# Branch A's values: both halves of V in one stationary operand, half the rows moved and added afterwards

## The reference, cut to what matters

```python
qa, ka = apply_rope(qa), apply_rope(ka)
o_a, _ = banded_attention(qa, ka, va, A_WINDOW - 1, sink=sinks)       # softmax over at most 128 keys
y_a = ((o_a * silu(gate_a)) @ w_pa)
y_b = ((o_b * silu(gate_b)) @ w_pb)                                   # branch B, dilated attention
merged = sigmoid(mg_a + b_gate[0]) * y_a + sigmoid(mg_b + b_gate[1]) * y_b
out = layer_norm(DN_ALPHA * x + merged @ w_out, ln_g, ln_b)
```

## Time and profile before

| | |
|---|---|
| time, median of 3 runs | 1389.39 us (1388.9 to 1390.16) |
| the profiled execution's own time | 1388.75 us |
| its span, from the first to the last instruction | 1387.0 us |
| mean granted TensorE clock | 0.997 |
| PE, DVE, ACT, POOL busy | 98%, 34%, 41%, 48% of the span |

### The profile page before, as it was taken

The page is one execution under the profiler, slowest core; times in us unless marked ns, Lnnn a source line. Parts: engine busy times, 40 slices in busy tenths (PEclk is TensorE's granted clock), DMA queues, the critical chain, the costliest instruction groups (busy, mean ns, idle before and its releaser), DMA issues.

```text
span 1387.0 us, 19876 instructions
## 1 busy us (share of the span) xinstructions
PE 1360.5 (98%) x6488; PEld 1154.3 (83%) x6488; DVE 477.4 (34%) x846; ACT 574.5 (41%) x971; POOL 669.8 (48%) x512
## 2 busy tenths in 40 slices
PE   9999999999999999999999999999999999999996
PEld 7888888778988988898898888888888888888884
DVE  5866565652031223203111011010101202287688
ACT  5455464543472365347237322222222222445442
POOL 4633443454555545455454465464555636422214
PEclk9999999999999999999999999999999999999998
DMA  8432241435374354337434343653536446377664
GB/s 260 131 122 76 76 136 52 130 111 119 93 168 137 87 120 135 119 92 163 147 110 137 88 149 113 151 129 102 177 91 157 122 130 147 95 248 259 208 241 152
DMA packets 204990, 190.07 MB, mean 137 GB/s; under 512 B 16528, under 2 KB 178576, under 8 KB 204944
## 3 DMA queue, kind: packets, MB, share of 16 engines
q1 hardware_dynamic: 191344, 151.74, 37.1%
q0 software_dynamic: 13600, 37.75, 11.0%
HBM read 185.23 MB, written 41.94 MB: 164 GB/s over the span
## 4 chain that ended last, share of the span: by engine, by line
PE 50%; issue 25%; POOL 20%; DVE 2%; ACT 1%; DMA 1%; POOLq 0%; SPq 0%; DVEq 0%; ACTq 0%
PE acc L1493 45%; POOL w_lo L574 11%; POOL w_lo L573 9%; PE ps_scores L1493 2%; PE ps_out L1493 1%; PE ps_turn L1493 1%; PE ps_out L1582 0%; DMA raw<-xT 0%; DMA raw<-w_in 0%; DVE w_lo L1290 0%; POOL q_left L599 0%; POOL q_left L601 0%; DVE x_lo L981 0%; DVE z L1351 0%; ACT both_stats L655 0%
## 5 line engine op out<-in xcount | busy, mean ns | idle before, releaser
L573 POOL TENSOR_TENSOR w_lo<-raw,w_hi 128x512 fp32r<-128x512 f32 x241 | 319.3, 1325 | 700.8 <-ACT w_hi L627 577.3
L1493 PE MATMUL acc<-x_hi,w_hi 128*128 128x512 f32 x1216 | 478.2, 393 | 5.8 <-POOL w_lo L574 3.2
L1493 PE MATMUL acc<-x_hi,w_lo 128*128 128x512 f32 x1216 | 474.2, 390 | 0.0
L1493 PE MATMUL acc<-x_lo,w_hi 128*128 128x512 f32 x1216 | 474.1, 390 | 0.0
L627 ACT ACTIVATE w_hi<-raw 128x1024 fp32r<-128x1024 f32 x224 | 234.5, 1056 | 337.2 <-PE acc L1493 332.5
L574 POOL TENSOR_TENSOR w_lo<-raw,w_hi 128x512 fp32r<-128x512 f32 x241 | 332.4, 1379 | 0.0
L1493 PEld LDWEIGHTS acc<-x_hi,w_hi 128*128 128x128 f32 x1216 | 228.5, 188 | 51.2 <-POOL w_lo L574 3.9
L1493 PEld LDWEIGHTS acc<-x_hi,w_lo 128*128 128x128 f32 x1216 | 228.2, 188 | 48.3
L1493 PEld LDWEIGHTS acc<-x_lo,w_hi 128*128 128x128 f32 x1216 | 228.5, 188 | 44.1
L1216 DVE TENSOR_TENSOR part_a<-acc,part_a 128x512 f32<-128x512 f32 x16 | 11.1, 691 | 321.7 <-PE acc L1493 321.7
L1493 PE MATMUL acc<-w_hi,x_lo 128*128 128x384 f32 x256 | 85.6, 334 | 0.0
(11 more groups left out here) (265 smaller groups left out, 1621.3 us busy)
## 6 DMA issues: line engine op xcount, KB each, us to landing
raw<-w_in SPq DMA_DIRECT2D x384, 128.0 KB, 2.3
q_left<-w_out POOLq DMA_DIRECT2D x12, 2048.0 KB, 13.6
raw<-w_in SPq DMA_DIRECT2D x256, 96.0 KB, 2.5
raw<-q_left SPq DMA_DIRECT2D x32, 512.0 KB, 4.8
raw<-w_in SPq DMA_DIRECT2D x64, 192.0 KB, 2.9
raw<-w_pa SPq DMA_DIRECT2D x64, 128.0 KB, 6.2
raw<-w_out SPq DMA_DIRECT2D x16, 512.0 KB, 4.2
raw<-xT SPq DMA_DIRECT2D x8, 512.0 KB, 4.7
```

The source lines that it names most:

```text
L573: nc.gpsimd.tensor_tensor(dst[:, left], raw[:, slot, left], hi[:, left].bitcast(F32), ALU.subtract)
L1493: ins = nc.tensor.matmul(into[:, 0:cols], s, m, start=start and k == 0, stop=stop and k == n - 1)
```

## The change

Branch A's values no longer sit twice in a stationary operand. `v_pair` holds, in its 128 columns, the rounded half of the 64 channels and beside it the remaining half. One matmul with a piece of the probabilities gives the rounded half's product in rows 0 to 63 and the remaining half's in rows 64 to 127. Two passes follow each other, over `probsT_hi` and over `probsT_lo`, instead of three matmuls for each block of keys; the wait for `probsT_lo` moves between the passes. The result is the sum of the upper and the lower rows. ACT copies, for each head of the pair, the 64 rows that lie on the wrong side into `across` (`move_halves`, at the plan's "values"), DVE adds the rows that lie on the right side, and then multiplies by the gate, 128 x 128 at once. The product lo x lo is now contained too.

```diff
-        v_hi_a, v_lo_a = (at(n, branch_at + where, [P, 4, A_KV, P], F32R)
-                          for n, where in (("v_hi_a", 8192), ("v_lo_a", 12288)))
+        v_pair = at("v_pair", branch_at + 8192, [P, 4, A_KV, P], F32R)
+        across = at("across", branch_at + 12288, [P, 2, P])
...
+        def v_part(c):
+
+            return v_pair.rearrange("p b v (c d) -> p (b v) c d", c=2)[:, :, c, :]
 
         def turned_v():
-
-            return ps_turn.rearrange("p (n d) -> p n d", d=A_DH).unsqueeze(2).to_broadcast([P, 8, 2, A_DH])
+            return ps_turn.rearrange("p (n d) -> p n d", d=A_DH)
...
+            def move_halves(u, a):
+
+                act.wait_ge(out_psum, a + 1)
+                if u > 1:
+                    act.wait_ge(gated_a, a - 1)
+                for hh in range(2):
+                    main, rest = (slice(A_DH * n, A_DH * n + A_DH) for n in (hh, 1 - hh))
+                    last = nc.scalar.activation(across[main, u % 2, :], ps_out[rest, hh * P:hh * P + P], ACT.Copy)
+                last.then_inc(halves_moved, 1)
...
+                    if stage == "values" and kind == "a":
+                        move_halves(u, first_unit + u)
...
-                        nc.scalar.activation(twice(v_hi_a), turned_v(), ACT.Copy).then_inc(v_hi_ready, 1)
+                        nc.scalar.activation(v_part(0), turned_v(), ACT.Copy).then_inc(v_hi_ready, 1)
...
             def gate_out(kind, u, a, i):
 
-                dve.wait_ge(out_psum, a + 1)
+                dve.wait_ge(halves_moved, a + 1)
                 j, b = divmod(u, 4)
                 for hh in range(2):
-                    g = gate_a[half[hh], j, b * P:(b + 1) * P]
-                    last = nc.vector.tensor_tensor(g, ps_out[half[hh], hh * P:hh * P + P], g, ALU.mult)
+                    whole = across[half[hh], u % 2, :]
+                    last = nc.vector.tensor_tensor(whole, ps_out[half[hh], hh * P:hh * P + P], whole, ALU.add)
                 last.then_inc(out_gated, 1)
+                dve.wait_ge(out_gated, a + 1)
+                g = gate_a[:, j, b * P:(b + 1) * P]
+                nc.vector.tensor_tensor(g, across[:, u % 2, :], g, ALU.mult).then_inc(gated_a, 1)
                 if b == 3 and j == 1:
-                    dve.wait_ge(out_gated, a + 1)
+                    dve.wait_ge(gated_a, a + 1)
                     split_gated(kind, gate_a[:, j, :], i + A_ITERS * j, i * 2 + j)
...
-            nc.vector.tensor_tensor(twice(v_lo_a), turned_v(), twice(v_hi_a).bitcast(F32), ALU.subtract).then_inc(v_a_ready, 1)
+            nc.vector.tensor_tensor(v_part(1), turned_v(), v_part(0).bitcast(F32), ALU.subtract).then_inc(v_a_ready, 1)
...
                         if kind == "a":
-                            pe.wait_ge(probsT_rest, a + 1)
                             if u:
                                 pe.wait_ge(out_gated, a)
...
-                            for kb in kbs:
-                                for n, (v, p) in enumerate(((v_hi_a, probsT_hi), (v_hi_a, probsT_lo), (v_lo_a, probsT_hi))):
-                                    last = nc.tensor.matmul(ps_out[:, 0:2 * P], v[:, b - 1 + kb, j, :],
+                            for p in (probsT_hi, probsT_lo):
+                                if p is probsT_lo:
+                                    pe.wait_ge(probsT_rest, a + 1)
+                                for kb in kbs:
+                                    last = nc.tensor.matmul(ps_out[:, 0:2 * P], v_pair[:, b - 1 + kb, j, :],
                                                             p[:, 2 * kb:2 * kb + 2, :].rearrange("p c q -> p (c q)"),
-                                                            start=kb == kbs[0] and n == 0, stop=kb == 1 and n == 2)
+                                                            start=p is probsT_hi and kb == kbs[0], stop=p is probsT_lo and kb == 1)
```

More of the change, by code:

```diff
@@ L335, in build @@
         out_psum, out_gated = sem("out_psum"), sem("out_gated")
+        halves_moved, gated_a = sem("halves_moved"), sem("gated_a")
         collected, weighed, near_spread, mixed = sem("collected"), sem("weighed"), sem("near_spread"), sem("mixed")
@@ L364, in by_residue @@
             return t.rearrange("p (r b j) -> p r b j", b=4, r=NR)
-        def twice(t):
-            return t.rearrange("p b v (c d) -> p (b v) c d", c=2)
+        def v_part(c):
+            return v_pair.rearrange("p b v (c d) -> p (b v) c d", c=2)[:, :, c, :]
         def turned_v():
-            return ps_turn.rearrange("p (n d) -> p n d", d=A_DH).unsqueeze(2).to_broadcast([P, 8, 2, A_DH])
+            return ps_turn.rearrange("p (n d) -> p n d", d=A_DH)
         def slot_o(q):
@@ L1134, in attend @@
                 if kind == "a" and g == 15:
-                    dve.wait_ge(out_gated, first_unit + A_UNITS // 2)
+                    dve.wait_ge(gated_a, first_unit + A_UNITS // 2)
                     split_gated(kind, gate_a[:, 0, :], i, i * 2)
```

## The result

The changed kernel takes 1400.51 us (median of 6 runs, 1396.54 to 1402.64), the kernel before 1389.73 us (6 runs, 1388.9 to 1390.16) beside it: ratio 1.0075, 95% interval 1.006 to 1.009, slower. The profiled execution took 1400.09 us, with a span of 1398.3 and a mean granted clock of 0.992, where it was 0.997. The forecast was 1395.4 us, slower: right in sign, inside its range, 5.1 us too low.

The account below looks back on a forecast made before the run. PE, busy 98% of 1387 us, was taken as the bound. Terms -5.9 (matmuls), +9.0 (stage ends), +2.4 (DVE stalls) and +0.5 (fourth stage's end) gave +6.0 us: 1389.39 becomes 1395.4, range 1389 to 1403.5.

Parts of the forecast that it names:

- matmuls, with unit 0's wait: Branch A's values on PE: 46 matmuls save 5.4 us, one more per stage inside unit 0's wait 0.5; together -5.9.
- units 2 and 3, hand-over: DVE late after units 0 and 1, stalling PE: +2.4 us over four stages; fourth stage's end, towards branch B: +0.5.
- three stage ends: DVE's gate waits for ACT's late copy of unit 7, scores 3.0 us later per end: +9.0 us (6.0 to 12.3).
- rival +6: Clock falls to 1.2 GHz after PE's idle time at three stage ends, 2 us each: 1401.4; chance 22%.
- What comes off PE: Branch A's values: 56 fewer matmuls at 0.117 us, ten at stage ends not counted, leaving 46, 5.4 us.
- The hand-over: Fourth stage's end, where branch B takes over: later gate and new multiplication delay the rotary work, +0.5 us (0 to 1.4).
- the last rival: Faster: ACT's late copy at stage ends is hidden and unit 7's matmuls count, -6.6 us, 1382.8; chance 9%.
- the first rival: PE idle about 3.4 us before three stages lowers the clock, 2 us lost each: 1401.4 (to 1406); chance 22%.
- The second rival: VectorE binds the units: multiplication meets POOL at most units, stalls reach 1.7 us per stage: 1399.8; chance 8%.
- No change and faster: Stage ends: chain free of POOL, 1389.9, no change, chance 11%; or ACT's copy hidden, 1382.8, faster, chance 9%.
- the late chain: DVE's delayed work at stage ends runs free of POOL: +2.0 us per end, +0.5 in all, 1389.9; chance 11%.

Follow-up runs that it names:

- e1: Changed kernel without ACT's move and DVE's addition, the halves not summed, only the 56 fewer matmuls kept: 1382.96 us, ratio 0.9953 to the kernel before.
- e6: Changed kernel with unit 7 of each stage gated as before, without move and addition, its halves not summed: 1386.71 us, ratio 0.9983 to the kernel before.
- e3: Changed kernel with 32 unused transposes of the identity on PE during the wait at each of three stage ends: 1395.66 us, ratio 1.0046 to the kernel before.
- e5: Changed kernel with unit 7's move ahead of bank 0's swap and the two q_low operations at blocks 7 and 10 instead of 5 and 8: 1386.88 us.
- e2: Changed kernel with unit 7's move put ahead of bank 0's swap in ScalarE's queue at three stage ends: 1389.08 us, ratio 0.9996 to the kernel before.
- e10: Changed kernel with unit 7's move between bank 0's swap and the next `high` in ScalarE's queue: 1396.77 us, ratio 1.0051 to the kernel before.
- e4: Changed kernel with a third value pass, the rounded probabilities again, and the wait ahead of all passes: 1402.3 us, ratio 1.0091 to the kernel before.

## Why the prediction came out as it did

| term | predicted | measured | from |
|---|---|---|---|
| matmuls, with unit 0's wait | -5.9 | -6.6 | e1 - before |
| units 2 and 3, hand-over | +2.4 + 0.5 | +3.75 | e6 - e1 |
| three stage ends | +9.0 | +8.95 | e3 - e6 |
| the clock | 0, rival +6 | +4.85 | changed - e3 |
| sum | +6.0 | +11.0 | beside its own kernel before: +10.8 |

By the starts the four terms are -7.2, +4.4, +8.8 and +4.8, together +10.8.

- **What comes off PE**: right in kind, 0.7 short. The step failed by which unit 7's six matmuls "don't count", since "what follows there is set by DVE": DVE's chain begins with the result of those matmuls. In e1 the stages that end this way shrink by 1.9, and its -6.6 us is what the last rival gives if unit 7's matmuls count.
- **Units 2 and 3**: DVE's lateness came where it was placed, but once in a stage: at unit 2 in three of them, at unit 3 in the fourth. By starts the recorded 2.2 us are 0.6 in each of the three and 1.2 in the fourth, 3.0 in all; of the 0.8 by which e6's three stages are longer than e1's, 0.2 remain unplaced.
- **The hand-over**: mis-sized by little. Stage 4 is 0.5 longer in e3 than before, with 14 fewer matmuls, of which the prediction lets 10 count; it holds the fourth `probs_a` wait of 0.9 and a new one of 1.2 for `shifted`, against 0.4 less for `q_a`. The table parts them: e5, without the `probs_a` wait, is still 0.9 longer in stage 4 than e1 (52.9 and 52.0). That is the hand-over, with what little the other units lose there; 0.5 was predicted.
- **The stage ends**: the step that decided, right in place and in size: PE waits 3.28 us, 3 to 3.6 were predicted. By starts 58.7 - 55.8 = 2.9 per end, 3.0 predicted; ACT's two copies 0.54, the 0.55 predicted; the multiplication 0.41 and the cast 1.27 beside POOL, as the chain had it. e2 and e10 show that it was the place in ScalarE's queue.
- **The clock**: the step that failed. "The mechanism at a stage's end with the clock up gets 50%" against 22% for its fall. With the clock up (e3) the kernel takes 1395.66, 0.3 from the forecast, which is partly luck: 0.7 too little taken off and 0.85 too little put on cancel. As it is, the first rival's 1401.4 is nearer to 1400.51. The second rival's 1399.8 is near it too, but by a mechanism that didn't happen: with stalls of 1.7 us per stage and the hand-over's 0.5 it needs 7.3 us where e6 - e1 is 3.75. The row of before that spoke for a fall after some 2.4 idle us at the kernel's end held for the stage ends, idle for 3.3: it should have carried more than the lack of a case inside the stages. But idle time alone doesn't settle it: one of e4's waits of 3.06 us passed without a fall. The rule cited from the Trainium skill (TensorE: Matmul & The Clock Gate, "HAM oscillation"), by which idle gaps bring the lower rate, agrees with the windows at 0.50 here. The loss per end, guessed at 2 us, was 1.6 on average.
- **No change and faster**: the late chain did meet POOL, and ACT's copy was not hidden. e2 shows the other side: with the delay at 0.9 us per end, just under the 1.0 from which the prediction let a gain begin, the kernel comes out level.

## What to carry to other kernels

Saving instructions on the busiest engine pays only until the new hand-over meets an in-order queue: ask what stands ahead of the new step there, at the one place where the receiver has no slack, and exempt that place (here one unit of eight; with one step moved on DVE it turned +10.8 us into -4.6). Price a new idle time of PE twice, once for its length and once for the clock behind it. Compare the starts of the same instruction over stages rather than adding up waits.

## What the runs showed of the hardware

- The clock stayed at 1.00 with PE waiting 1.2 us at the ends (e2) and up to 1.5 (e5), and fell at each of three waits of 2.6 (e10) and of 3.3 (changed kernel), but only at two of three of 3.06 (e4). It fell during the wait or up to 0.9 us after PE had started again. The loss for nearly the same idle time ranged from 1.2 to 2.3 us per stage in the changed kernel, and from none to 2.6 in e10.
- Transposes of the identity, 0.109 us apart, kept the granted clock at 1.00 (e3).
- Two ACT copies 64 x 128 out of PSUM, shifted by 64 partitions, take 0.271 us each, against 0.598 for 128 x 512: fewer elements per partition help much less than in proportion.
- POOL's job costs DVE wherever it falls: 1.27 for a cast of 0.43 in the changed kernel, 1.58 for a subtraction of 0.69 in e10. DVE's chain from the additions to the scores took 7.9 us in the one and 8.2 in the other, so that e10's start, 0.9 us sooner, gave back only 0.7.
